# Expert stage of a transformer trunk: two steps of 1792 columns with 7 KB weight units in place of four steps with 8 KB units

## The chip, the core and the metric

One core of a Trainium2 chip runs the whole program. The time is device microseconds of that core from the first to the last work of one execution; lower is better.

## The reference

A small trunk of two layers works on 256 tokens of 1024 numbers, all in float32: a recurrent layer with a dense feed-forward block, then an attention layer with a block of eight experts. Only the expert block is touched by the change:

```python
def moe_swiglu(h, router, w_gate, w_up, w_down):
    logits = (t @ router).astype(jnp.float32)
    top_v, top_i = lax.top_k(logits, TOP_K)                  # TOP_K = 2 of 8
    w = jax.nn.softmax(top_v, axis=-1)
    combine = jnp.sum(jax.nn.one_hot(top_i, N_EXPERTS) * w[..., None], axis=1)
    for e in range(N_EXPERTS):
        out = out + combine[:, e:e + 1] * swiglu(t, w_gate[e], w_up[e], w_down[e])
# swiglu(h, ...) = (silu(h @ w_gate) * (h @ w_up)) @ w_down
# w_gate, w_up: 1024 x 3584 per expert; w_down: 3584 x 1024; 352 MB for all eight
```

## The kernel before

All eight experts' weights are read once, whatever the routing. The experts are sorted by how many tokens chose them and worked on in pairs, one large ("heavy", job 0, up to 128 tokens) beside one small ("light", job 1, up to 64 tokens). There are four such groups here: `OPENING`, `SECOND`, one turn of a loop and `last`. `gather` collects the tokens of a pair by matmuls with one-hot matrices (`xg_hi`, `xg_lo` for the heavy expert, `xl` for the light one), `scatter` adds the weighted results back into `X`.

Weights come in units of 1 MiB (128 partitions x 2048 floats), 42 per expert and 84 per group. SyncE issues the loads (`load`, L461) into a ring of `RING` = 10 slots in an order fixed by `pair_table`; a load waits until TensorE has used up the unit that was in its slot (`used`). A unit of the heavy expert is split: ScalarE copies it rounded into `whi` (`hi_to`, L555, three places), VectorE writes the rest into `lows` (`lo_to`, L1562), and TensorE runs three matmuls per tile, hi x hi, lo x hi and hi x lo (`heavy_unit`, L1380 to L1382). A unit of the light expert is used straight from the ring in full float32; its 64 token columns take half of the array, and the two column halves `g` = 0, 1 alternate (`light_unit`, L1394).

The 3584 hidden columns are done in `PAIRS` = 4 steps of 1024, 1024, 1024 and 512 (`PAIR_W`). Step p computes gate (G) and up (U), multiplies silu(gate) by up (`silu`, `product`), transposes the result on TensorE (`act_transposes` L1356, `light_transposes` L1363, reading every second column through `paired_rows`) and uses it in the down projection (D) of the next step; `act_T_hi` and `act_T_lo` bring the transposes into `aT_hi` and `aT_lo`. Units alternate two light, two heavy (`turns`). In a load of gate or up each partition reads rows of 4 KB (2 KB in the last step), in a load of down 8 KB. The down sums stay in PSUM over the whole group: banks 0 and 1 for the heavy expert, bank 2 for the light one. The heavy gate and up sums use banks 4 and 5, the light ones 6 and 7, the transposes 0, 1, 3, 4 and 5.

At the end of a group `gather` runs for the next one, `light_rows` (L2045) adds the two halves of `xl`, and `y_to_hi` and `y_to_lo` bring the results to SBUF for the scatter.

Of the kernel before, what the change touches and what calls it, by code (L numbers as in the profile page):

```python
# [22 lines left out]
P = 128  # L23
# [31 lines left out]
assert TURNS * RING == PAIR_UNITS + PAIR_UNITS // SKIP and FFN_UNITS % SPLIT == 0  # L55
# [19 lines left out]
PAIRS = 4  # L75
PAIR_W = [2 * CW, 2 * CW, 2 * CW, CW]
PAIR_U = [w // CW * 2 for w in PAIR_W]


def turns(steps, jobs=(1, 0)):  # L80

    for b in range(0, len(steps), RUN):
        for job in jobs:
            for n in steps[b:b + RUN]:
                yield job, n


def pair_table(opening=False):

    units, place = [], {}

    def stage(kind, p, steps, jobs=(1, 0)):
        width = D if kind == "D" else PAIR_W[p]
        tiles = UK * CW // width
        row, col = (p * 2 * UK, 0) if kind == "D" else (0, p * 2 * CW)
        for job, n in turns(steps, jobs):
            place[kind, job, p, n] = len(units)  # L100
            units.append((job, "GUD".index(kind), row + n * tiles, col, width))

    for p in range(PAIRS):
        steps = range(PAIR_U[p])
        if p == 0 and opening:
            for kind, job, few in OPENING_STEPS:
                stage(kind, p, few, (job,))
            continue
        stage("G", p, steps)
        if p:  # L110
            stage("D", p - 1, range(0, 2))
        stage("U", p, steps)
        if p:
            stage("D", p - 1, range(2, PAIR_U[p - 1]))
    stage("D", PAIRS - 1, range(PAIR_U[PAIRS - 1]), (0, 1))
    assert len(units) == PAIR_UNITS == len(place)
    return units, place


OPENING_STEPS = (("G", 0, range(4)), ("G", 1, range(2)), ("U", 0, range(4)), ("G", 1, range(2, 4)),  # L120
                 ("U", 1, range(4)))
# [11 lines left out]
PLACES = (2, 3, 4, 5, 9, 7, 0, 1, 8, 6)  # L133
# [16 lines left out]
class Group:  # L150
# [18 lines left out]
    def unit(self, kind, job, p, n):  # L169
        return self.place[kind, job, p, n % PAIR_U[p]]  # L170
# [5 lines left out]
    def split(self, n):  # L176
        return at(N_MOE + self.ahead * FFN_UNITS + n, FFN_UNITS, self.i)
# [18 lines left out]
HEAVY_DONE = PLACE["D", 0, PAIRS - 1, PAIR_U[PAIRS - 1] - 1] + 1  # L196
# [8 lines left out]
def hybrid_trunk(nc, x, norm_mix, norm_ffn, lru_w_in, lru_conv_w, lru_conv_b, lru_w_a, lru_b_a, lru_w_x, lru_b_x,  # L205
                 lru_log_lambda, lru_w_out, fox_w_in, fox_b_f, fox_q_gain, fox_k_gain, fox_w_out, ffn_w_gate,
                 ffn_w_up, ffn_w_down, moe_router, moe_w_gate, moe_w_up, moe_w_down, out):
    with ExitStack() as ctx:
# [8 lines left out]
        with ExitStack() as w3:  # L217
            ring = sb("ring", [P, RING, UK * CW], where=w3)
        with ExitStack() as w4:
            lows = sb("lows", [P, RING, UK * CW], F32R, where=w4)  # L220
# [6 lines left out]
        with ExitStack() as l3:  # L227
            yl_hi, yl_lo = (sb(s, [P, CW], F32R, where=l3) for s in ("yl_hi", "yl_lo"))
            sb("yl_gap", [P, D], where=l3)
            xl = sb("xl", [P, KT, HD], where=l3)  # L230
        sb("rows3_home", [P, 3 * D])
# [66 lines left out]
        with ExitStack() as a4:  # L298
            with ExitStack() as t4:
                aT_hi = sb("aT_hi", [P, 2, 2 * UK, P], F32R, where=t4)  # L300
                aT_lo = sb("aT_lo", [P, 2, 2 * UK, P], F32R, where=t4)
            sb("aT_home", [P, 4 * D], where=a4)
# [4 lines left out]
            gt = sb("gt", [P, 2 * CW], where=a4)  # L307
            gl = sb("gl", [P, CW], where=a4)
            S = sb("S", [P, TT, 2 * P], F32R, where=a4)
            ST = sb("ST", [P, 2, T], F32R, where=a4)  # L310
            tk = sb("tk", [P, 12, TT, E], where=a4)
            aTl = sb("aTl", [P, 2, 2 * UK, HD], where=a4)
# [16 lines left out]

        def light_T(p):  # L330

            return aTl[:, p % 2, 0:PAIR_W[p] // P].rearrange("p (g a) s -> p a g s", g=2)

        def light_T_bank(p):

            return ps[:, 3, 0:PAIR_W[p] // 2].rearrange("p (a g s) -> p a g s", g=2, s=HD)

# [5 lines left out]

        T_BANK = (0, 4)

# [31 lines left out]
        m_xs, l_silu, l_act, l_T, l_copied = (sem(s) for s in ("m_xs", "l_silu", "l_act", "l_T", "l_copied"))  # L377
# [48 lines left out]
        def _(sp):  # L426
# [28 lines left out]
            def load(group, i, expert):  # L455
                job, matrix, row, col, width = group.table[i]
                tiles = UK * CW // width
                src = expert_w[matrix][expert, row * P:(row + tiles) * P, col:col + width
                                       ].rearrange("o (p k) n -> p (o k) n" if width == D and matrix == 2 else
                                                   "o (k p) n -> p (o k) n", p=P)  # L460
                sp.dma_start(ring[:, slot(i)].rearrange("p (k n) -> p k n", k=tiles), src  # L461
                             ).then_inc(arrived[slot(i)], 16)

            for i in AHEAD:
                n = last_dense(slot(i))
                if slot(i) < RR:
                    sp.wait_ge(lo_done, n)
                else:
                    sp.wait_ge(used, n + 1)
# [66 lines left out]
        def _(act):  # L536
            nxt = [1]

            def hi_to(n, group=None):
# [10 lines left out]
                while nxt[0] < FFN_UNITS and group.heavy[nxt[0]] <= n:  # L550
# [4 lines left out]
                    nc.scalar.activation(whi[:, rounded(q)], ring[:, slot(i)], ACT.Copy).then_inc(hi_done, 1)  # L555
# [239 lines left out]
            def both(bank, n=2 * CW):  # L795
                return ps[:, bank:bank + 2].rearrange("p b n -> p (b n)")[:, 0:n]

# [12 lines left out]
            def y_to_hi(job, done, weighed):  # L810
                act.wait_ge(used, done)
                act.wait_ge(m_ST, weighed)
# [1332 lines left out]
```

## Time and profile before

| | before |
|---|---|
| time, median of 3 (lowest to highest) | 1362.03 us (1360.93 to 1363.13) |
| the profiled execution, its own time | 1364.23 us |
| its span from first to last instruction | 1362.5 us |
| TensorE matmul busy | 97% of the span |
| VectorE, ScalarE busy | 54%, 46% |
| data read from memory | 433 MB |
| granted TensorE clock | 0.998 of full |

The expert stage begins with the first gather at 493 us and ends with the output at 1362 us. Matmuls are pipelined, so one of 390 ns can start every 227 ns; a distance between starts is read from the first column of the timeline, a busy time includes the overlap only once.

### The profile page before, as it was taken

Reading aid. Unit: us, or ns where it says so; the run is one execution under the profiler, and the core shown is the slowest. Engines: PE = TensorE matmul, PEld = TensorE weight load, DVE = VectorE, ACT = ScalarE, POOL = GpSimd, SP = SyncE. Lnnn points to the kernel's source line nnn. Section 1 sums busy time; section 2 is a strip of 40 time slices with the busy share of each in tenths; the row PEclk is TensorE's granted clock in tenths of the full one; section 3 lists DMA queues with packets and bytes.
Section 4 is the critical chain, followed back from the end, with each engine's and each line's share of the span. In section 5 each row is a group of like instructions: output and inputs, shape, how many; then the busy total and the mean of one; then the engine's idle time right before and its main releaser. Section 6 shows DMA issues by size and latency. Waiting matters only on the chain.

```text
span 1362.5 us, 16077 instructions
## 1 busy us (share of the span) xinstructions
PE 1324.5 (97%) x6430; PEld 935.8 (69%) x6430; DVE 736.3 (54%) x632; ACT 629.7 (46%) x573; POOL 29.0 (2%) x34
## 2 busy tenths in 40 slices
PE   9999999999999999999999999999999999999998
PEld 8978888888888875565666556575556656665665
DVE  6975444445654574554555554555545555455455
ACT  5855334444456463434444444444444444453443
POOL 2000000000310000000000000000000000000000
PEclk9999999999999999999999999999999999999999
DMA  9556555654543449999999999999999999999995
GB/s 333 170 181 218 192 192 189 193 189 126 184 144 124 164 173 366 414 415 410 403 413 409 393 413 413 405 412 409 403 409 412 407 411 409 411 400 414 411 401 230
DMA packets 127881, 434.79 MB, mean 319 GB/s; under 512 B 6960, under 2 KB 9120, under 8 KB 113472
## 3 DMA queue, kind: packets, MB, share of 16 engines
q1 hardware_dynamic: 127344, 433.11, 82.9%
q8 instruction: 51, 0.84, 0.3%
q0 software_dynamic: 368, 0.63, 0.2%
q14 instruction: 22, 0.18, 0.0%
q10 hardware_dynamic: 96, 0.03, 0.0%
HBM read 432.69 MB, written 1.05 MB: 318 GB/s over the span
## 4 chain that ended last, share of the span: by engine, by line
PE 73%; DMA 15%; DVE 5%; ACT 4%; issue 1%; SPq 1%; DVEq 0%; POOL 0%; ACTq 0%
PE ps L1394 15%; DMA ring<-in_moe_w_gate_dram 9%; PE ps L918 9%; PE ps L920 9%; PE ps L919 9%; PE ps L1380 9%; PE ps L1381 8%; PE ps L1382 8%; DMA ring<-in_moe_w_up_dram 4%; DVE lows L1562 2%; DMA ring<-in_moe_w_down_dram 2%; ACT whi L555 2%; PE ps L1325 1%; DVE wlo L1555 1%; SPq L461 1%
## 5 line engine op out<-in xcount | busy, mean ns | idle before, releaser
L1562 DVE TENSOR_TENSOR lows<-ring,whi 128x2048 fp32r<-128x2048 f32 x168 | 383.1, 2290 | 256.9 <-ACT whi L555 256.8
L555 ACT ACTIVATE whi<-ring 128x2048 fp32r<-128x2048 f32 x168 | 320.3, 1912 | 324.5 <-DMA ring<-in_moe_w_up_dram 120.7
L1394 PE MATMUL ps<-ring,xl 128*64 128x512 f32 (+1 forms) x1024 | 204.1, 544 | 5.0 <-DVE xl L2045 3.4
L1555 DVE TENSOR_TENSOR wlo<-raw,whi 128x2048 fp32r<-128x2048 f32 x73 | 166.5, 2288 | 73.9 <-PE ps L920 71.8
L1380 PE MATMUL ps<-whi,hT_hi 128*128 128x512 f32 x444 | 179.3, 404 | 13.5 <-DVE lows L1562 13.0
L547 ACT ACTIVATE whi<-raw 128x2048 fp32r<-128x2048 f32 x73 | 139.4, 1917 | 85.9 <-PE ps L920 82.9
L1381 PE MATMUL ps<-lows,hT_hi 128*128 128x512 f32 x444 | 173.3, 390 | 0.0
L1382 PE MATMUL ps<-whi,hT_lo 128*128 128x512 f32 x444 | 173.0, 390 | 0.0
L918 PE MATMUL ps<-whi,hT_hi 128*128 128x512 f32 x384 | 152.9, 398 | 3.2 <-DVE wlo L1555 1.4
L920 PE MATMUL ps<-whi,hT_lo 128*128 128x512 f32 x384 | 149.7, 390 | 0.0
L919 PE MATMUL ps<-wlo,hT_hi 128*128 128x512 f32 x384 | 149.5, 389 | 0.0
L1394 PEld LDWEIGHTS ps<-ring,xl 128*64 128x64 f32 x1024 | 69.1, 136 | 116.0 <-issue 107.9
L1380 PEld LDWEIGHTS ps<-whi,hT_hi 128*128 128x128 f32 x444 | 83.3, 188 | 67.4 <-issue 26.4
L1394 PE MATMUL ps<-ring,aTl 128*64 128x512 f32 x448 | 102.3, 598 | 0.0
L1380 PE MATMUL ps<-whi,aT_hi 128*128 128x512 f32 x224 | 91.2, 407 | 5.7 <-DVE lows L1562 5.7
L1382 PEld LDWEIGHTS ps<-whi,hT_lo 128*128 128x128 f32 x444 | 83.3, 188 | 18.0
L1381 PEld LDWEIGHTS ps<-lows,hT_hi 128*128 128x128 f32 x444 | 83.5, 188 | 15.2
L1382 PE MATMUL ps<-whi,aT_lo 128*128 128x512 f32 x224 | 87.6, 391 | 0.0
L1381 PE MATMUL ps<-lows,aT_hi 128*128 128x512 f32 x224 | 87.4, 390 | 0.0
L918 PEld LDWEIGHTS ps<-whi,hT_hi 128*128 128x128 f32 x384 | 72.2, 188 | 19.0 <-issue 3.1
L920 PEld LDWEIGHTS ps<-whi,hT_lo 128*128 128x128 f32 x384 | 72.1, 188 | 15.3
L919 PEld LDWEIGHTS ps<-wlo,hT_hi 128*128 128x128 f32 x384 | 72.2, 188 | 13.8
(318 smaller groups left out, 1318.7 us busy)
## 6 DMA issues: line engine op xcount, KB each, us to landing
ring<-in_moe_w_gate_dram SPq DMA_DIRECT2D x112, 1024.0 KB, 11.9
ring<-in_moe_w_up_dram SPq DMA_DIRECT2D x112, 1024.0 KB, 13.4
ring<-in_moe_w_down_dram SPq DMA_DIRECT2D x112, 1024.0 KB, 13.9
raw<-in_fox_w_in_dram SPq DMA_DIRECT2D x16, 1024.0 KB, 5.2
raw<-in_ffn_w_gate_dram SPq DMA_DIRECT2D x14, 1024.0 KB, 5.2
raw<-in_ffn_w_up_dram SPq DMA_DIRECT2D x14, 1024.0 KB, 5.1
raw<-in_ffn_w_down_dram SPq DMA_DIRECT2D x14, 1024.0 KB, 5.1
raw<-in_lru_w_in_dram SPq DMA_DIRECT2D x8, 1024.0 KB, 10.2
```

The lines of the kernel that those rows point to most:

```text
L461: sp.dma_start(ring[:, slot(i)].rearrange("p (k n) -> p k n", k=tiles), src).then_inc(arrived[slot(i)], 16)
L547: nc.scalar.activation(whi[:, m % HR], raw[:, m % RR], ACT.Copy).then_inc(hi_done, 1)
L555: nc.scalar.activation(whi[:, rounded(q)], ring[:, slot(i)], ACT.Copy).then_inc(hi_done, 1)
L918: mm(dst(t), hi, whi[:, m % HR, k * CW:(k + 1) * CW], start=first and k == 0, stop=False)
L919: mm(dst(t), hi, wlo[:, m % LR, k * CW:(k + 1) * CW], start=False, stop=False)
L920: ins = mm(dst(t), lo, whi[:, m % HR, k * CW:(k + 1) * CW], start=False, stop=last and k == UK - 1)
L1380: mm(ps[:, bank + h], hi, w_hi[:, cols], start=first and k == 0, stop=False)
L1381: mm(ps[:, bank + h], hi, w_lo[:, cols], start=False, stop=False)
L1382: ins = mm(ps[:, bank + h], lo, w_hi[:, cols], start=False, stop=last and k == tiles - 1)
L1394: ins = mm(ps[g * HD:(g + 1) * HD, bank, 0:half], src(k), ring[:, slot(i), cols], start=first and k == 0, stop=last and k == tiles - 1, sk ...
L1555: nc.vector.tensor_tensor(wlo[:, m % LR], raw[:, m % RR], whi[:, m % HR].bitcast(F32), ALU.subtract).then_inc(lo_done, 1)
L1562: nc.vector.tensor_tensor(lows[:, slot(i)], ring[:, slot(i)], whi[:, rounded(q)].bitcast(F32), ALU.subtract).then_inc(lo_done, 1)
```

## The change

The hidden columns are done in `PAIRS` = 2 steps of `WIDE` = 1792. Every unit has 7 KB per partition (`ring` is 11 slots x 1792 floats): 48 units per expert, 96 per group. A gate or up unit is one tile of 128 rows x 1792 columns, so each partition reads one run of 7 KB. For down, a partition takes seven neighbouring rows of 896 (28 KB in one piece), and a unit is a quarter of it; the activations are therefore transposed at every seventh column (`every_seventh`) in place of every second.

Gate and up of the heavy expert fill four banks with 448 columns each (4 to 7), the light expert uses 2 and 3. Down matmuls are cut at bank and unit edges (`down_pieces`): three of 512 columns and one of 256 per unit. Since the light banks are shared, the light down sums are brought to SBUF three times in a group and added up in `yl` by VectorE (`light_sum`). The order of units, of the waits and of VectorE's and ScalarE's operations around them is written anew. `light_rows` moves into the last down step. `ST`, `gl`, `aT_hi` and `aT_lo` get new places in SBUF.

```diff
-PAIR_UNITS = 2 * FFN_UNITS
-RING, SPLIT, RUN = 10, 3, 2
-SKIP = 14
+PAIRS = 2
+NU = 8
+WIDE = F // PAIRS
+HALF = WIDE // 2
+BW = WIDE // 4
+RW = HALF // P
+EXPERT_UNITS = PAIRS * 3 * NU
+PAIR_UNITS = 2 * EXPERT_UNITS
+RING, SPLIT, RUN = 11, 3, 2
+SKIP = 32
...
+def down_pieces(u):
+    cuts = [u * WIDE, (u + 1) * WIDE] + [c for c in range(0, RW * D, CW) if u * WIDE < c < (u + 1) * WIDE]
+    edges = sorted(set(cuts))
+    return [(c // D, c % D, e - c, c - u * WIDE) for c, e in zip(edges, edges[1:])]
...
+        stage("G", 0, range(NU), HEAVY_FIRST)
+        stage("U", 0, range(NU), HEAVY_FIRST)
+    stage("G", 1, range(NU), LIGHT_FIRST)
+    stage("D", 0, DOWN_A, LIGHT_FIRST)
+    stage("U", 1, range(NU), HEAVY_FIRST)
+    stage("D", 0, DOWN_B, HEAVY_FIRST)
+    stage("D", 1, range(NU), HEAVY_FIRST)
...
             def load(group, i, expert):
+                if kind == "D":
+                    rows = p * WIDE + n // 4 * HALF
+                    src = w[expert, rows:rows + HALF, :].rearrange("o (q r) n -> q (o r n)", r=RW)
+                    src = src[:, n % 4 * WIDE:(n % 4 + 1) * WIDE]
+                else:
+                    src = w[expert, n * P:(n + 1) * P, p * WIDE:(p + 1) * WIDE].rearrange("o p n -> p (o n)")
...
-            def paired_rows(src, a):
-                return src[:, a // 2 * 2 * P:(a // 2 + 1) * 2 * P].rearrange("p (q two) -> p two q", two=2)[:, a % 2]
+            def every_seventh(src, b, a):
+                return src[:, b * HALF:(b + 1) * HALF].rearrange("p (q r) -> p r q", r=RW)[:, a]
...
+                for h in range(4):
+                    cols = slice(h * BW, (h + 1) * BW)
+                    dst = ps[:, 4 + h, 0:BW]
+                    mm(dst, xg_hi[:, n], w_hi[:, cols], start=n == 0, stop=False)
+                    mm(dst, xg_hi[:, n], w_lo[:, cols], start=False, stop=False)
+                    ins = mm(dst, xg_lo[:, n], w_hi[:, cols], start=False, stop=n == NU - 1)
...
+            def light_down(group, p, n):
+                for a, c, width, at_col in down_pieces(n % 4):
+                    g = c // CW
+                    ins = mm(ps[g * HD:(g + 1) * HD, 2 + p, c % CW:c % CW + width], aTl[:, in_half(p, b), a],
+                             ring[:, slot(i), at_col:at_col + width], start=a == 0 and (p == 0 or b == 0),
+                             stop=a == RW - 1 and (p == 0 or b == 1), skip_group_check=True)
...
+            def light_sum(group, part):
+                p, n = ((0, DOWN_A[-1]), (0, DOWN_B[-1]), (1, NU - 1))[part]
+                dve.wait_ge(used, group.units(group.unit("D", 1, p, n) + 1))
+                if part == 0:
+                    nc.vector.tensor_copy(yl[:], ps[:, 2]).then_inc(l_sum, 1)
+                else:
+                    dve.wait_ge(l_sum, group.nth(part, 3))
+                    nc.vector.tensor_tensor(yl[:], ps[:, 2 + p], yl[:], ALU.add).then_inc(l_sum, 1)
...
+                lo_to(unit("G", 0, 1, 0), group)
+                act_T_lo(group, 0)
+                if group is not OPENING:
+                    accumulate(1, group)
+                    lo_to(unit("G", 0, 1, 5), group)
+                    if following is not None:
+                        one_hot(group)
+                lo_to(unit("D", 0, 0, 2), group)
+                light_sum(group, 0)
+                lo_to(unit("D", 0, 0, 4), group)
+                product(group, 1)
+                light_product(group, 1)
+                lo_to(unit("D", 0, 0, 6), group)
+                act_T_lo(group, 1)
+                lo_to(unit("D", 0, 1, 1), group)
+                light_sum(group, 1)
+                if following is not None:
+                    lo_to(unit("D", 0, 1, 4), group)
+                    light_rows(following)
```

## Rows read from the trace of the kernel before

**Rows 1.** The page: busy times of the engines and the 40 slices.
```profile
PE 1324.5 (97%) x6430; PEld 935.8 (69%) x6430; DVE 736.3 (54%) x632; ACT 629.7 (46%) x573; POOL 29.0 (2%) x34
DMA  9556555654543449999999999999999999999995
```
**Rows 2.** Four stretches between gathers: from:to, length, PE busy (instructions), clock, DMA share, GB/s.
```profile
493.29:697.00 203.71, 196.50 (x922) 1.00 1.00 394
697.00:912.42 215.42, 209.66 (x972) 1.00 1.02 408
912.42:1128.60 216.18, 210.42 (x975) 1.00 1.02 408
1128.60:1357.00 228.40, 222.62 (x1032) 1.00 0.97 386
```
**Rows 3.** Waits of PE from 540 us on, and of ACT from 759 to 975.
```profile
PE ps L1380 <- DVE lows L1562: 18.7, 23, 1.4
PE ps L1394 <- DVE xl L2045: 3.4, 2, 1.7
...
ACT whi L555 <- DMA ring<-in_moe_w_up_dram: 30.2, 10, 6.2
ACT whi L555 <- DMA ring<-in_moe_w_down_dram: 25.6, 10, 5.5
ACT whi L555 <- DMA ring<-in_moe_w_gate_dram: 22.6, 8, 6.0
```
**Rows 4.** Stretches by packet size (2, 2, 8, 8, 4 KB): busy times, clock, share, GB/s.
```profile
861.00:869.00 8.00, 8.00 (x42) 4.96 (x39) 5.68 (x3) 4.03 (x4) 0.00 (x0) 1.00 1.05 387
884.00:892.00 8.00, 7.14 (x36) 4.97 (x34) 3.77 (x2) 1.80 (x2) 0.00 (x0) 1.00 1.06 389
872.00:880.00 8.00, 7.71 (x50) 5.66 (x47) 4.59 (x2) 3.19 (x3) 0.00 (x0) 1.00 1.02 420
897.00:913.00 16.00, 15.74 (x73) 10.80 (x73) 9.89 (x7) 8.42 (x6) 0.00 (x0) 1.00 1.01 418
936.00:964.00 28.00, 28.00 (x127) 16.39 (x126) 14.71 (x13) 10.95 (x8) 0.00 (x0) 1.00 1.03 409
```
**Rows 5.** Timeline of PE: start us, length us, instruction; dense 512, light 512/256, gather.
```profile
724.08 0.50 PE L1380 MATMUL ps<-whi,hT_hi 128*128 128x512 f32 x1
724.42 0.40 PE L1381 MATMUL ps<-lows,hT_hi 128*128 128x512 f32 x1
...
860.76 3.65 PE L1394 MATMUL ps<-ring,aTl 128*64 128x512 f32 x16
...
871.51 3.67 PE L1394 MATMUL ps<-ring,xl 128*64 128x256 f32 x32
...
878.07 0.39 PE L1382 MATMUL ps<-whi,hT_lo 128*128 128x512 f32 x1
...
880.79 0.39 PE L1382 MATMUL ps<-whi,hT_lo 128*128 128x512 f32 x1
...
912.42 2.08 PE L1316 MATMUL ps<-S,hn_hi 128*128 128x256 f32 x16
914.34 0.40 PE L1380 MATMUL ps<-whi,aT_hi 128*128 128x512 f32 x1
```
**Rows 6.** Transposes, step 1 (L960) and 2 (L1356): loads min/median/max ns; then starts.
```profile
L960 PEld LDWEIGHTS ps<-ident,X x48: 138/141/148, 87.8 to 482.4; 128*128 128x128 f32 x48
L1356 PEld LDWEIGHTS ps<-ident,gt x112: 195/209/219, 539.1 to 1342.0; 128*128 128x128 f32 x112
...
481.90 0.49 PE L960 MATMUL ps<-ident,X 128*128 128x128 f32 x3
482.01 0.49 PE L960 MATMUL ps<-ident,X 128*128 128x128 f32 x3
...
867.82 0.52 PE L1356 MATMUL ps<-ident,gt 128*128 128x128 f32 x3
867.94 0.52 PE L1356 MATMUL ps<-ident,gt 128*128 128x128 f32 x3
```
**Rows 7.** Groups by shape (busy us, mean ns), 759 to 975; then one wait of PE.
```profile
L1562 DVE TENSOR_TENSOR lows<-ring,whi 128x2048 fp32r<-128x2048 f32 x42 | 95.7, 2290 | 64.4 <-ACT whi L555 64.4
L2026 DVE TENSOR_TENSOR gt<-gt,ps 128x1024 f32<-128x1024 f32 x3 | 3.7, 1222 | 12.8 <-PE ps L1382 12.8
L2039 DVE TENSOR_TENSOR gl<-gl,ps 128x512 f32<-128x512 f32 x3 | 2.1, 685 | 2.3 <-PE ps L1394 2.3
L2045 DVE TENSOR_TENSOR xl<-ps,xl 128x512 f32<-128x512 f32 x1 | 0.7, 683 | 0.0
...
979.69 0.50 PE L1380 MATMUL ps<-whi,hT_hi 128*128 128x512 f32 x1 [1.33 <-DVE lows L1562]
```

More of the change, by code:

```diff
@@ L549, in hi_to @@
                     return
-                while nxt[0] < FFN_UNITS and group.heavy[nxt[0]] <= n:
+                while nxt[0] < EXPERT_UNITS and group.heavy[nxt[0]] <= n:
                     q, i = nxt[0], group.heavy[nxt[0]]
@@ new lines, in heavy_down @@
+            def heavy_down(group, p, n):
+                i = group.unit("D", 0, p, n)
+                b = n // 4
+                w_hi, w_lo = heavy_halves(group, i)
+                pe.wait_ge(lo_done, group.split(group.heavy.index(i)))
+                for a, c, width, at_col in down_pieces(n % 4):
+                    hi, lo = aT_hi[:, in_half(p, b), a], aT_lo[:, in_half(p, b), a]
+                    cols = slice(at_col, at_col + width)
+                    dst = ps[:, c // CW, c % CW:c % CW + width]
+                    mm(dst, hi, w_hi[:, cols], start=p == b == a == 0, stop=False, skip_group_check=True)
+                    mm(dst, hi, w_lo[:, cols], start=False, stop=False, skip_group_check=True)
+                    ins = mm(dst, lo, w_hi[:, cols], start=False, stop=p == b == 1 and a == RW - 1,
+                             skip_group_check=True)
+                ins.then_inc(used, 1)
@@ L1496, in pair @@
-                pe.wait_ge(l_copied, group.nth(PAIRS, PAIRS))
-                pe.wait_ge(m_tlo, group.nth(PAIRS, PAIRS))
-                if following is not None:
-                    gather(following, 0)
-                for job, n in turns(range(2), (0, 1)):
-                    down_unit(group, job, PAIRS - 1, n)
-                    if following is not None and job == 0 and n == 0:
+                    first_step(group)
+                act_transposes(group, 0)
+                light_transposes(group, 0)
@@ new lines, in pair @@
+                if group is not OPENING:
+                    pe.wait_ge(m_acc, group.twice(1))
+                    scatter(1)
+                for job, n in turns(range(NU), LIGHT_FIRST):
+                    if n == 0:
+                        pe.wait_ge((m_tlo, l_copied)[job], group.nth(1, PAIRS))
+                    half_unit(group, "G", job, 1, n)
+                    if group is not OPENING and job == 1 and n == 5:
+                        pe.wait_ge(m_acc, group.twice(2))
+                        selection_transposes(group)
@@ new lines, in pair @@
+                for job, n in turns(DOWN_B, HEAVY_FIRST):
+                    if job == 1 and n == DOWN_B[0]:
+                        pe.wait_ge(l_copied, group.nth(2, PAIRS))
+                    down_unit(group, job, 0, n)
+                    if (job, n) == (0, DOWN_B[0]):
+                        light_transposes(group, 1)
+                    if (job, n) == (0, DOWN_B[1]):
+                        act_transposes(group, 1)
+                pe.wait_ge(m_tlo, group.nth(2, PAIRS))
+                for job, n in turns(range(NU), HEAVY_FIRST):
+                    down_unit(group, job, 1, n)
+                    if following is not None and (job, n) == (0, 1):
+                        gather(following, 0)
+                    if following is not None and (job, n) == (0, 3):
@@ L1558, in lo_to @@
                     return
-                while nxt[0] < FFN_UNITS and group.heavy[nxt[0]] <= n:
+                while nxt[0] < EXPERT_UNITS and group.heavy[nxt[0]] <= n:
                     q, i = nxt[0], group.heavy[nxt[0]]
@@ L2104, in _ @@
-            pair(SECOND, Group(0, 2))
+            pair(OPENING, None, SECOND)
+            pair(SECOND, OPENING, Group(0, 2))
             dve.wait_ge(counted, 1)
@@ L2107, in _ @@
             with dve.Fori(0, loops) as n:
-                pair(Group(n, 2), Group(n, 3))
+                pair(Group(n, 2), Group(n, 1), Group(n, 3))
             last = Group(loops, 2)
-            pair(last, None)
-            for job in range(2):
-                y_to_lo(job, last.twice(1 + job))
+            pair(last, Group(loops, 1), None)
+            y_to_lo(0, last.twice(1))
+            light_sum(last, 2)
+            y_to_lo(1, last.twice(2))
             for j in range(2):
```

462 lines of the change are left out of this document (199 added, 263 removed).

## The prediction

> **What bounds the kernel now.** I read the page first. TensorE is busy 97% of the span, and from about 530 us the DMA slices stand at 9 to the end [rows 1]. The reader should see two resources near their limit in the same stretch, the expert stage. So I split the stage at the four places where TensorE begins to gather for a pair of experts, and ask for busy time, DMA share and GB/s [rows 2]. The middle stretches take 215.4 and 216.2 us; TensorE works 209.7 and 210.4 of them and the DMA engines all of it, at 408 GB/s. The idle time of TensorE in the four stretches is 7.2 + 5.8 + 5.8 + 5.8 = 24.6 us. The waits name what ends it: 18.7 us of the whole span for `lows`, 3.4 us for `xl` [rows 3]. ScalarE's waits say who was behind most of the `lows`: in one period it waits 78 us for weights to land [rows 3]. So the stage runs at the DMA's pace, but a DMA that costs nothing could give back 24.6 us and no more: behind it stands TensorE with 210 us of work in 216.
>
> **The DMA side.** A unit is 1 MiB now, in packets of 4 KB per partition for gate and up, 2 KB in step 3, 8 KB for down. The rate goes with the packet [rows 4]: 387 to 389 GB/s where 2 KB packets land, 409 for 4 KB, 418 to 420 for 8 KB. One engine moves 64 KB of a unit: 2.70 us at 388 GB/s, 2.565 at 409. The 16 packets more cost 0.14 to 0.16 us, near 9.5 ns each, over a floor of 2.41 us; 8 packets would then take 2.49 us, 421 GB/s, as the rows show. A group has 48 gate/up units at 2.565, 8 at 2.71 and 28 down at 2.49: 214.5 us, near the measured 216. After the change there are 96 units of 7/8 the size, 8 packets each: 2.41 x 7/8 + 0.076 = 2.185 us, so 209.8 us a group. The weights come 4.7 us sooner, and the DMA falls just below TensorE's present work.
> The Trainium skill ("DMA: Bandwidth & Descriptors", Why small descriptors are slow) gives about 3 cycles of fixed overhead per packet. At its 850 MHz, 480 packets fewer per engine and group would save an estimated 1.7 us, not 4.7. The rows show nearly three times that overhead, and the sum goes by the rows.
>
> **What TensorE gains as work.**
> (a) Heavy units. The same columns go through, but gate and up in 448-column matmuls, and down in 512s with a 256 at a unit's edge. Dense 512-column matmuls start 2.72 us / 12 = 226.7 ns apart, 256-column ones (the gather) 1.92 / 16 = 120 ns [rows 5]. That is 0.417 ns a column plus 13.3 ns each. Matmuls of the heavy expert go from 504 to 576 a group, 288 more in all: 288 x 13.3 ns = +3.8 us.
> (b) Switches between the two experts. The first matmul after a switch costs 0.1 us extra (724.08 to 724.42 against 0.23; [rows 5]). 40 switches become 45 per group: 20 x 0.1 = +2.0 us.
> (c) Light units. 16 instructions of 512 columns and 32 of 256 take the same 3.6 us [rows 5], so a narrower piece is free as long as the two column halves alternate. In down, eight cuts a group put two 256-column pieces on the same half one after the other. The trace has no such pair. If nothing overlaps there, one piece of 256 costs 0.21 us more, 8 x 4 x 0.21 = 6.8 us; the other end is 0. I take the middle, +3.4 us, having nothing nearer.
> (d) Transposes. There are 42 per group before and after, 168 in all. The operand that is loaded is read at every second column now, at every seventh afterwards. Rows exist for a step of 1 and of 2 [rows 6]: the load takes 141 and 209 ns, and starts of transposes lie 0.11 and 0.12 us apart, since the load hides behind its neighbour. A step of 7 is in no row. Below: 0 (a step of 2 already reads one number at a time; nothing suggests a gain). Above: the load grew by 67 ns on the doubling from 1 to 2; if the next doubling costs 134 and then no more, the load takes 343 ns and is what paces: +134 ns x 168 = 22.5 us. I take 20 ns each, +3.4 us, near the lower end, because the starts moved by only 10 ns when the load grew by 67.
> (e) Tail. The small expert's last sum now passes VectorE before ScalarE reads it (`light_sum`, 512 columns): +0.7 us by the 512-column `xl` addition [rows 7], with nothing beside it at the end.
> What stays: the gathers, the scatters, the number of transposes, the front up to 493 us. The waits for `xl` go (3.4 us of the 24.6): `light_rows` moves from the end of the group to the middle of the last down step, some 10 us before TensorE needs it.
>
> **What stays as waiting.** VectorE's operations get longer. By its 1024- and 512-column rows (1222 and 685 ns, [rows 7]) one of 1792 columns takes 2.03 us, and a `lows` unit shrinks from 2.29 to 2.02. I laid out its queue at the three seams. After step 0 the product (2.03), the light product (1.09), one `lows` and `act_T_lo` fit under the two light units (3.1), the transposes (2.4) and the scatter (2.4): slack of a microsecond, where it costs 1.33 us now (the wait at 979.69, [rows 7]). In the first down half `light_sum` (0.7) stands ahead of a `lows` (2.02) that is due in 2.4 us: 0.3 late. In the second half the same chain is even with its due time, and `act_T_lo` makes the last `lows` 0.4 late. That is about 1 us a group, 4 in all. The DMA, 3.2 us a group below TensorE's new work, adds perhaps 0.5 in three groups and 1 in the opening, where the landed units are used up first: 6.5 us remain of the 24.6.
>
> **The sum.** -24.6 + 6.5 + 3.8 + 2.0 + 3.4 + 3.4 + 0.7 = -4.8 us. The profiled execution took 1364.2 us (span 1362.5), 2.2 above the median. 1364.2 - 4.8 = 1359.4; against the median of 1362.0, 1357.2 us. A middle group should take 209.9 + (3.8 + 2.0 + 3.4 + 3.4)/4 + 1.5 = 214.5 us.
>
> **Rivals.**
> B, the slower side: the step of 7 sets the pace of the transposes. Place: `act_transposes` and `light_transposes`, all on TensorE, which nothing covers. It decides against the change from about 50 ns per transpose. At 134 ns: 1357.2 + 22.5 - 3.4, less 2.5 of waits that the slower TensorE no longer meets: 1373.8 us, and 1377 with (c) in full. For it: the load already rose by 67 ns at a step of 2, to well above the 120 ns between starts. Against it: that rise hardly moved the starts.
> The Trainium skill ("SBUF — State Buffer", Specifications, the row on cachelines) says that at least two hits per 16-byte line are needed for full bandwidth. A step of 2 floats still has two hits, a step of 7 (28 bytes) one. By that rule B holds; the trace doesn't settle it, as its load rows slow down already where the rule says full bandwidth.
> C: VectorE or ScalarE becomes late at the seams, since long operations stand ahead of `lows` with slack near zero. 2.5 us more a group: 1367. Against it: both engines are only half busy [rows 1].
> D: (c) and (d) cost nothing and 3 us less waiting stays: 1357.2 - 6.8 - 3 = 1347.4.
> E, the change doesn't do what it says: 7 KB packets move no faster than the mix now (a 28 KB pitch between partitions, in no row). The period stays 216 with TensorE's additions inside it: 1363. Against it: the steady order 388, 409, 419 by packet size.
>
> **How the numbers follow.** Chances: A (the forecast) 0.42, B 0.30, C 0.08, D 0.10, E 0.10. Range: D's 1347.4 to B with (c) in full, 1377, a microsecond more for an error of the sum: 1347 to 1378, which leaves out the ends of B and D and unforeseen waits. A measurement of this kernel can tell about 0.2%, 2.7 us, from no change. A spreads from 1352 to 1363: 0.32 faster, 0.09 same, 0.01 slower. D is faster (0.10); E is same (0.09) or slower (0.01); C and B are slower (0.37), 0.01 of B same. Together: faster 0.42, same 0.19, slower 0.39. Both signs hold much; A's own range is 1352 to 1363.
>
> **What would show it.** DMA side right: packets of 7 KB alone, 418 to 421 GB/s wherever the queues are full, and a DMA share under 1.00 in the middle stretches. (a): heavy starts 200 ns apart. (c): 16 light instructions in 3.14 us, a down pair up to 0.2 us longer at each cut. (d): the load of `gt` near 209 to 230 ns and starts near 0.12 to 0.14 us, or for B above 300 ns and 0.25 us. Waits of TensorE: no `xl`, `lows` under 2 us a group. The forecast is wrong if TensorE's work in a middle stretch leaves 212 to 215 us, or if the share of the DMA stays at 1.02 over 216 us.

## The result and the profile after

| | before | after |
|---|---|---|
| median (lowest to highest), 20 runs each | 1362.55 us (1360.88 to 1366.74) | 1364.89 us (1364.55 to 1366.27) |
| after / before, with its 95% interval | | 1.0018 [1.0011, 1.0025] |
| span of the profiled execution | 1362.5 us | 1363.1 us |

The kernel after is 0.18% slower. Its interval lies above 1, so the direction is clear of noise, but it is too little to matter: the prediction took 0.2% as what can be told from no change. The forecast was 1357.2 us, 0.35% faster. Behind the small number two large ones cancel. The page of the kernel after shows it first (busy times; the chain that ended last; the landing of the weight loads in us); [rows 1] has before:

```profile
PE 1346.0 (99%) x6782; PEld 986.7 (72%) x6782; DVE 744.3 (55%) x644; ACT 630.1 (46%) x565; POOL 28.9 (2%) x34
...
PE 92%; DVE 4%; ACT 2%; DMA 1%; issue 1%; SPq 0%; DVEq 0%; ACTq 0%
...
ring<-in_moe_w_gate_dram SPq DMA_DIRECT2D x128, 896.0 KB, 8.4
ring<-in_moe_w_up_dram SPq DMA_DIRECT2D x128, 896.0 KB, 8.9
ring<-in_moe_w_down_dram SPq DMA_DIRECT2D x128, 896.0 KB, 10.1
```

TensorE works 1346.0 us where it worked 1324.5: 21.5 us more, in a span that hardly moved. The stretches between gathers say where. They answer [rows 2]; the boundary is the first matmul of the gather, and the first and last stretch have other ends than before, since the gather now stands in another place among the down units. Columns: from:to, length, TensorE busy (instructions), granted clock, DMA share, GB/s.

```profile
492.44:675.93 183.49, 181.32 (x912) 1.00 0.99 401
675.93:892.35 216.42, 216.32 (x1065) 1.00 1.01 411
892.35:1108.79 216.44, 216.34 (x1065) 1.00 1.00 408
1108.79:1357.80 249.01, 248.53 (x1213) 1.00 0.93 378
```

The four lengths sum to 865.4 us, against 863.7 before. The idle time of TensorE in them is 2.2 + 0.1 + 0.1 + 0.5 = 2.9 us, against 24.6: 21.7 us of waiting went. Its work is 862.5 us, against 839.2: 23.3 us of work came. A middle group has 216.3 us of work where it had 209.7 and 210.4, and idles for 0.1 us. Its length, 216.4 us, is within 1 us of what it was (215.4 and 216.2). The waits of TensorE from 540 us on, which answer [rows 3], are down to two; `lows` and `xl` are gone:

```profile
PE ps L1434 <- ACT aTl L879: 1.7, 1, 1.7
PE ps L1369 <- DVE yl_lo L2068: 0.4, 1, 0.4
```

The DMA did what was forecast. Two stretches in which its queues were full (all five engines' busy times, clock, share, GB/s), beside [rows 4]:

```profile
604.00:612.00 8.00, 8.00 (x40) 5.27 (x40) 3.96 (x2) 5.04 (x4) 0.00 (x0) 1.00 1.02 422
618.00:640.00 22.00, 22.00 (x108) 15.68 (x108) 12.54 (x7) 10.21 (x6) 0.00 (x0) 1.00 1.02 419
```

7 KB packets move at 419 to 422 GB/s, where 418 to 421 was forecast. Over a whole group it is 408 to 411. That is TensorE's pace: a group's 88.1 MB in its 216.4 us are 407 GB/s, and a load waits until TensorE has freed its slot.

So the question is why TensorE has 5.9 to 6.7 us more work in a middle group, where the forecast had 3.15. The timeline has the answer in two places. Gate and up, then down; each time 16 instructions of the light expert (two units) and the first matmul of the heavy one behind them. A matmul of the light expert leaves two records in the trace, so x16 are eight matmuls:

```profile
631.40 3.23 PE L1434 MATMUL ps<-ring,xl 128*64 128x448 f32 x16
634.56 0.47 PE L1422 MATMUL ps<-whi,hT_hi 128*128 128x448 f32 x1
...
639.62 3.23 PE L1434 MATMUL ps<-ring,xl 128*64 128x448 f32 x16
...
688.33 3.65 PE L1464 MATMUL ps<-ring,aTl 128*64 128x512 f32 x16
691.91 0.50 PE L1451 MATMUL ps<-whi,aT_hi 128*128 128x512 f32 x1
...
696.98 3.65 PE L1464 MATMUL ps<-ring,aTl 128*64 128x512 f32 x16
```

Two light units of gate or up take 634.56 - 631.40 = 3.16 us. Two light units of down take 691.91 - 688.33 = 3.58 us, for the same 7 KB each. It is what two units of 8 KB took before, x16 and 3.65 us long in [rows 5] too. A whole turn (two light, two heavy) is 639.62 - 631.40 = 8.22 us for gate and up and 696.98 - 688.33 = 8.65 us for down. The turn before was 9.25 us (light blocks at 785.28 and 794.53 in its timeline), and 7/8 of that is 8.09.

### The profile page after: what moved, and what is told of

Read it like the earlier page. It is cut to its first block, busy times and chain, and to the rows that moved or that the text cites. A ratio compares the mean times of both kernels' runs of the same rounds, so it can differ in the third digit from the quotient of the medians.

```text
span 1363.1 us, 16877 instructions
## 1 busy us (share of the span) xinstructions
PE 1346.0 (99%) x6782; PEld 986.7 (72%) x6782; DVE 744.3 (55%) x644; ACT 630.1 (46%) x565; POOL 28.9 (2%) x34
## 4 chain that ended last, share of the span: by engine, by line
PE 92%; DVE 4%; ACT 2%; DMA 1%; issue 1%; SPq 0%; DVEq 0%; ACTq 0%
PE ps L1434 15%; PE ps L962 9%; PE ps L964 8%; PE ps L963 8%; PE ps L1464 8%; PE ps L1422 8%; PE ps L1424 8%; PE ps L1423 8%; PE ps L1451 4%; PE ps L1452 4%; PE ps L1453 4%; PE ps L1369 1%; PE ps L1399 1%; DMA raw<-in_lru_w_in_dram 1%; DVE wlo L1613 1%; PE ps L1360 1%
## 5 line engine op out<-in xcount | busy, mean ns | idle before, releaser
L1620 DVE TENSOR_TENSOR lows<-ring,whi 128x1792 fp32r<-128x1792 f32 x192 | 386.2, 2023 | 270.6 <-ACT whi L603 270.4
L603 ACT ACTIVATE whi<-ring 128x1792 fp32r<-128x1792 f32 x192 | 324.4, 1698 | 296.0 <-PE ps L1424 130.8
L1434 PE MATMUL ps<-ring,xl 128*64 128x448 f32 x1024 | 205.9, 545 | 1.7 <-ACT aTl L879 1.7
L1422 PE MATMUL ps<-whi,hT_hi 128*128 128x448 f32 x508 | 191.7, 377 | 0.0
L1424 PE MATMUL ps<-whi,hT_lo 128*128 128x448 f32 x508 | 185.6, 365 | 0.0
L1423 PE MATMUL ps<-lows,hT_hi 128*128 128x448 f32 x508 | 185.5, 365 | 0.0
L962 PE MATMUL ps<-whi,hT_hi 128*128 128x512 f32 x384 | 152.9, 398 | 3.2 <-DVE wlo L1613 1.4
L964 PE MATMUL ps<-whi,hT_lo 128*128 128x512 f32 x384 | 149.7, 390 | 0.0
L1464 PE MATMUL ps<-ring,aTl 128*64 128x512 f32 (+1 forms) x512 | 116.7, 545 | 0.0
L1451 PE MATMUL ps<-whi,aT_hi 128*128 128x512 f32 (+1 forms) x256 | 97.6, 381 | 0.4
```

What stands on the lines that cost most here:

```text
L603: nc.scalar.activation(whi[:, rounded(q), 0:WIDE], ring[:, slot(i)], ACT.Copy).then_inc(hi_done, 1)
L962: mm(dst(t), hi, whi[:, m % HR, k * CW:(k + 1) * CW], start=first and k == 0, stop=False)
L964: ins = mm(dst(t), lo, whi[:, m % HR, k * CW:(k + 1) * CW], start=False, stop=last and k == UK - 1)
L1422: mm(dst, xg_hi[:, n], w_hi[:, cols], start=n == 0, stop=False)
L1423: mm(dst, xg_hi[:, n], w_lo[:, cols], start=False, stop=False)
L1424: ins = mm(dst, xg_lo[:, n], w_hi[:, cols], start=False, stop=n == NU - 1)
```

## The experiments

Every kernel was timed beside the kernel before on the same chip; ratios are to those runs. "The changed kernel" is the one under test, 1.0018. The edits are shown in part; "..." marks what is left out.

**Theory 1: narrow beside wide.** The prediction's step (c) spoke of 256-column pieces on the same half of the array one behind the other. The first theory was that a lone piece, which has no neighbour of its own length, costs the 0.44 us. `alt_halves` orders the light pieces so that the halves alternate all through, by a table `light_pieces` that cuts one 512 more in each pair of units in two:

```diff
-                for a, c, width, at_col in down_pieces(n % 4):
+                for a, c, width, at_col in light_pieces(n % 4):
...
```

> The changed kernel with only the order and cutting of the light expert's down matmuls altered: beside each 256-column piece its partner on the other column half is cut to 256 too, so that halves of equal width alternate; columns, sums and loads are the same. Theory 1 (a 256-column piece beside a 512-column one on the other half costs as much as a 512-column one, 0.44 us per cut, 32 cuts): a light down pair falls from 3.58 to 3.14 us, a middle group from 216.4 to about 213, the whole by 13 to 14 us, to a ratio near 0.992 against the kernel before. If the DMA (209.8 us a group) takes over part, 0.994. Rival (the extra TensorE work lies in the 448-column matmuls and the switches, the cut is nearly free): the pair stays above 3.5 us and the ratio at 1.001 to 1.002.

Measured: 1365.95 us, ratio 1.0014 [1.0005, 1.0023]. The pair (now nine matmuls, x18) takes 605.40 - 601.82 = 3.58 us as before the edit:

```profile
601.82 3.65 PE L1473 MATMUL ps<-ring,aTl 128*64 128x512 f32 x18
605.40 0.50 PE L1460 MATMUL ps<-whi,aT_hi 128*128 128x512 f32 x1
```

Theory 1 fell: this order of the pieces, in which the halves alternate, changes nothing. What is left is how many columns each half gets. A partition's quarter of 28 KB is 1792 floats, 1.75 rows of 1024, and two units are 3.5 rows. Columns 0 to 511 of a row go to half 0, columns 512 to 1023 to half 1. So one half gets four pieces of 512 in a pair of units and the other three, and in the next pair it is the other way round. **Theory 2:** a block of light matmuls lasts as long as the half with more columns. Then 4 x 512 columns in one half cost what the pairs of 2048-column units cost before (4 x 512 in both halves), 3.58 us; balanced, it would be 7/8 of that, 3.13. That is 0.44 us x 8 pairs x 4 groups = 14 us.

**Turns of four.** Over four light down units both halves get seven pieces of 512, so theory 2 says 6.3 us in place of 7.16. `alt_run4` makes all turns four units long, gate and up too, on top of the edit of `alt_halves`:

```diff
-RING, SPLIT, RUN = 11, 3, 2
+RING, SPLIT, RUN = 11, 3, 4
```

> The same as alt_halves, and units of one expert follow each other in runs of four in place of two (the one constant RUN). Theory 1 with switches at 0.1 us each: about 22 switches fewer per group, 88 in all, 9 us below alt_halves if the units land in time; the DMA's 209.8 us a group is then the next limit, so a middle group of 210 to 211 us and a ratio near 0.987. Rival: four heavy units in a row outrun ScalarE and VectorE (1.70 and 2.02 us a unit against 2.43) or the DMA, waits for the lower halves return, and it is no faster than alt_halves or slower.

Measured: 1390.4 us, ratio 1.0199 [1.0184, 1.0213]. The block behaves as theory 2 says (`828.95 6.24`, 36 instructions), but TensorE now waits for VectorE and ScalarE, whose operations were laid out for turns of two, and behind the longest waits the granted clock falls as well (0.66 from 790 to 800 us; 0.984 over the whole run).

```profile
PE ps L1460 <- DVE lows L1629: 20.7, 11, 2.8
PE ps L1443 <- ACT aTl L888: 14.8, 4, 4.1
...
828.95 6.24 PE L1473 MATMUL ps<-ring,aTl 128*64 128x512 f32 x36
```

`down_quads` takes turns of four light units in down only:

```diff
-def turns(steps, jobs):
+def turns(steps, jobs, run=RUN):
...
+def downs(steps, jobs):
+    if len(steps) == 4:
+        return list(turns(steps, jobs, 4)) if jobs == LIGHT_FIRST else [(0, 4), (0, 5), (1, 4), (1, 5), (1, 6), (1, 7),
+                                                                        (0, 6), (0, 7)]
+    return [(0, 0), (0, 1), (1, 0), (1, 1), (1, 2), (1, 3), (0, 2), (0, 3), (0, 4), (0, 5), (1, 4), (1, 5), (1, 6),
+            (1, 7), (0, 6), (0, 7)]
...
```

> The changed kernel, with the light expert's down units taken four in a row (a whole half of a step) in place of two; the loads follow the same new order, gate and up keep their pairs. Two down units are 3.5 rows of 1024 columns, so one column half of the array gets four 512-column matmuls and the other three, in the next pair the other way round; four units give seven to each. Theory 2 (the extra TensorE work in down is this imbalance, paid in full since the longer half sets the pace): light down takes 6.2 us for four units in place of 2 x 3.58, 1.0 us less four times a group, with the fewer switches 4 us a group; the whole 10 to 16 us faster than the change, ratio 0.990 to 0.994 against the kernel before, if no new wait comes. Theory 1 (narrow pieces) has already fallen. Rival: waits for the heavy lower halves or for landed units return with four in a row, and the ratio stays above 0.998.

Measured: 1369.51 us, ratio 1.0057 [1.0043, 1.0071], the wrong way. TensorE's work fell (1337.6 us against 1346.0), but in three of the groups it waits twice for a `lows`, 14.4 us in all, and behind five of these six waits the clock falls. Waits of TensorE, three windows of 10 us (clock last but two), and its timeline:

```profile
PE ps L1431 <- DVE lows L1629: 7.4, 3, 2.5
PE ps L1460 <- DVE lows L1629: 7.0, 3, 2.3
...
680.00:690.00 10.00, 10.00 (x57) 7.81 (x55) 3.09 (x2) 1.52 (x2) 0.00 (x0) 1.00 1.02 419
690.00:700.00 10.00, 7.65 (x33) 4.91 (x33) 7.14 (x5) 6.76 (x5) 0.00 (x0) 0.83 0.98 381
1130.00:1140.00 10.00, 7.65 (x40) 4.55 (x40) 8.47 (x5) 6.40 (x4) 0.00 (x0) 1.00 0.79 286
...
693.89 0.39 PE L1460 MATMUL ps<-whi,aT_hi 128*128 128x256 f32 x1 [2.35 <-DVE lows L1629]
...
695.28 0.63 PE L1461 MATMUL ps<-lows,aT_hi 128*128 128x512 f32 x1
695.71 0.63 PE L1462 MATMUL ps<-whi,aT_lo 128*128 128x512 f32 x1
...
696.56 0.63 PE L1461 MATMUL ps<-lows,aT_hi 128*128 128x512 f32 x1
696.99 0.63 PE L1462 MATMUL ps<-whi,aT_lo 128*128 128x512 f32 x1
```

From 695.28, 1.4 us after the wait, a matmul of 512 columns starts every 0.43 us in place of 0.23: the lower of the two clock levels. The granted clock of the window is 0.83. The third of the waits of 2.35 us, which ends at 1133.64, had no such fall: 1.00 from 1130 to 1140.

`quads_reordered` mends the place of the waits. In the last down step all heavy units but two stand before the last four light ones, and the next group's tokens come in one heavy unit later:

```diff
-    return [... (0, 4), (0, 5), (1, 4), (1, 5), (1, 6), (1, 7), (0, 6), (0, 7)]
+    return [... (0, 4), (0, 5), (0, 6), (0, 7), (1, 4), (1, 5), (1, 6), (1, 7)]
...
-                    hi_to(unit("D", 0, 1, 4), group)
+                    hi_to(unit("D", 0, 1, 5), group)
...
-                    lo_to(unit("D", 0, 1, 4), group)
+                    lo_to(unit("D", 0, 1, 5), group)
```

> down_quads with its seams mended: the last down step takes its heavy units as 2, then 6 in a row, and ends with four light ones again, and ScalarE and VectorE bring in the next pair's tokens after one heavy unit more, so that no heavy half waits behind them. Theory 2 (imbalance of the column halves, 1.0 us per four light down units): a middle group of 212 to 213 us in place of 216.4, no idle stretch above 1 us and so no fall of the granted clock; the whole 12 to 16 us below the change, ratio 0.990 to 0.993. Rival: six heavy units in a row meet late lower halves or late landings, and the ratio is 0.996 or more.

Measured: 1345.09 us, ratio 0.9875 [0.986, 0.989]. It beats both kernels. No wait for `lows` is left, and four light units take 680.67 - 674.46 = 6.21 us where two pairs took 7.16:

```profile
674.46 6.28 PE L1473 MATMUL ps<-ring,aTl 128*64 128x512 f32 x32
680.67 0.50 PE L1460 MATMUL ps<-whi,aT_hi 128*128 128x512 f32 x1
...
672.46:884.04 211.58, 211.58 (x1063) 1.00 1.01 419
```

A middle group is 211.6 us, 4.85 less than 216.4. Theory 2 explains 4 x 0.95 = 3.8 of it, and four blocks of the light expert in place of eight save eight switches between the experts, at 0.1 us 0.8. Since this kernel also changes the order of units, two more runs separate the causes.

**Balance alone.** `balanced_halves` leaves order, loads and turns, and deals the light columns to the halves in chunks of 256 by turns, so that a pair gives seven chunks to each (its columns come out in another order, another sum):

```diff
-                for a, c, width, at_col in down_pieces(n % 4):
-                    g = c // CW
-                    ins = mm(ps[g * HD:(g + 1) * HD, 2 + p, c % CW:c % CW + width], aTl[:, in_half(p, b), a],
-                             ring[:, slot(i), at_col:at_col + width], start=a == 0 and (p == 0 or b == 0),
+                for k in range(RW):
+                    a, c = divmod(n % 4 * RW + k, 4)
+                    g, half = c % 2, c // 2
+                    ins = mm(ps[g * HD:(g + 1) * HD, 2 + p, half * 2 * P:(half + 1) * 2 * P], aTl[:, in_half(p, b), a],
+                             ring[:, slot(i), k * 2 * P:(k + 1) * 2 * P],
+                             start=a == 0 and half == 0 and (p == 0 or b == 0),
```

> The changed kernel with one edit: the light down units are cut into seven pieces of 256 columns each, and the pieces go to the two column halves by turns (piece k of a quarter to half k mod 2), so that two units of a pair give 7 pieces to either half. Loads, order of units, waits and all heavy work stay. The light down results stand in another order of columns, so the output is another sum. Theory 2 (the longer half sets the pace: now 4 x 512 columns against 3 x 512 in each pair): the light down pair falls from 3.58 to 3.14 us, 8 pairs x 4 groups x 0.44 = 14 us less, ratio 0.991 to 0.992, middle group 212.9 us, and it takes half of what was gained by taking the down units in fours out of the comparison: the rest there is order and switches. Rival (a light unit of 7 KB costs this much however its columns stand, for instance by the ring read or by the switch of weights): pair stays at 3.58 and the ratio at 1.001 to 1.002.

Measured: 1352.64 us, ratio 0.9921 [0.9908, 0.9935]: the median is 12.3 us below that of the changed kernel, against 14 expected (12.0 below `seam_move`, timed beside it, which is as slow as the changed kernel). The pair falls to 690.45 - 687.27 = 3.18 us:

```profile
687.27 3.24 PE L1465 MATMUL ps<-ring,aTl 128*64 128x256 f32 x28
690.45 0.50 PE L1451 MATMUL ps<-whi,aT_hi 128*128 128x512 f32 x1
...
675.14:888.47 213.33, 213.24 (x1160) 1.00 1.01 417
```

A middle group falls by 3.1 us, to 213.3. 8 x (3.58 - 3.18) = 3.2. Theory 2 holds; the rival, that a 7 KB unit costs this much however its columns stand, fell. The narrower pieces are not what gives it: in gate and up 32 records of 256 columns and 16 of 512 take the same [rows 5], and the turns of four have pieces of 512.

**Seam alone.** `seam_move` makes only the second and third edit of `quads_reordered`.

> The changed kernel with one edit: at the last down stage ScalarE and VectorE bring in the next group's tokens one heavy unit later (after heavy unit 5 in place of 4), as in the kernel with down units in fours and their order mended. Order of units, matmuls and loads stay. The changed kernel waits only 2.9 us in the expert stage, none of it for these operations, so theory 2 expects no change: ratio 1.001 to 1.002 and a middle group of 216.4 us. Rival (the order of these operations is what gave the gain of the mended fours over the plain ones by itself): a gain of 1 us or more per group, ratio 0.999 or below.

Measured: 1364.68 us, ratio 1.0014 [1.0005, 1.0023]. The seam edit gives nothing by itself (a middle group is 216.4 us still), so the gain of `quads_reordered` over the changed kernel is in the order and length of the blocks.

**What the DMA costs.** Two kernels load only half of the columns of the small expert's units and multiply that half twice, so their results are another sum; the work of the engines stays. `before_thin` does it to the kernel before, `after_thin` to the changed one.

```diff
+                dst = ring[:, slot(i)]
+                if job == 1:
+                    dst, src = dst[:, 0:HALF], src[:, 0:HALF]
+                sp.dma_start(dst, src).then_inc(arrived[slot(i)], 16)
```

> The kernel before, with every load of the light expert carrying half its bytes (its matmuls read the loaded half twice, so part of the weights is left out); matmuls, waits and operations are the same in number and size. The DMA's work falls by a quarter, so what is left is TensorE with the waits that the DMA does not cause. Theory 1 (24.6 us of idle TensorE, of which all but the 1.3 us at each seam of ScalarE and VectorE come from landing): 1342 to 1346 us, ratio 0.985 to 0.988. Rival (the waits are made by the order on ScalarE and VectorE): above 1355 us.

> The changed kernel, with every load of the light expert carrying half its bytes (its matmuls read the loaded half twice, so part of the weights is left out). The same was measured on the kernel before: 22.5 us less. Theory (TensorE alone sets the pace of the change, 2.9 us of it idle in the expert stage): 0 to 3 us less than the change, so a ratio of 1.000 to 1.002, and about 22 us slower than the kernel before with the same thinning. Rival (the DMA still shares the pace): 6 us or more less than the change, below 0.998.

Measured: `before_thin` 1341.14 us, ratio 0.9835 [0.982, 0.985]; `after_thin` 1365.48 us, ratio 1.0023 [1.0013, 1.0034]. The DMA cost the kernel before 22.5 us (1363.61 beside it), and costs the changed one nothing that can be measured. The same stretches of `before_thin` (columns as in the result) show where they were:

```profile
492.61:689.60 196.99, 195.29 (x918) 1.00 0.85 304
689.60:900.42 210.82, 209.40 (x975) 1.00 0.87 315
900.42:1111.13 210.71, 209.38 (x976) 1.00 0.87 313
1111.13:1334.03 222.90, 221.58 (x1031) 1.00 0.79 288
```

The four are 841.4 us long, 22.3 less. Idle time went from 24.6 to 5.8 us (5.3 of it waits for `lows`, one of 1.3 in each group), so 18.7 of the 24.6 were the DMA's. The other 3.6 us went from TensorE's busy time, 839.2 to 835.6, though the matmuls are the same (in `after_thin` the same edit left it at 863 us): in the kernel before, the DMA also stretched what counts as work.

**Transposes.** `unit_step` reads neighbouring columns in place of every seventh, so the down projection gets the activations in another order (another sum).

```diff
-                return src[:, b * HALF:(b + 1) * HALF].rearrange("p (q r) -> p r q", r=RW)[:, a]
+                return src[:, b * HALF:(b + 1) * HALF].rearrange("p (r q) -> p r q", r=RW)[:, a]
```

> The changed kernel, with the transposes reading neighbouring columns in place of every seventh. This orders the activations otherwise than the down rows, so it is a timing experiment that computes another sum. Theory 1 (the step does not pace the transposes; loads took 216 ns against 209 at a step of 2): the load falls to 140 ns, the starts from about 0.12 to 0.11 us, the whole by at most 168 x 0.015 = 2.5 us. Rival B of the prediction in its full size would give back 20 us.

Measured: 1363.77 us, ratio 1.0001 [0.9992, 1.001], 1.1 us below the changed kernel's median, 2.3 by the ratios. The loads of `gt` (min/median/max ns) and a block of 14 transposes, the changed kernel first, then `unit_step` with a middle group:

```profile
L1399 PEld LDWEIGHTS ps<-ident,gt x112: 197/216/221, 563.2 to 1307.6; 128*128 128x128 f32 x112
...
873.24 1.87 PE L1399 MATMUL ps<-ident,gt 128*128 128x128 f32 x14
```

```profile
L1399 PEld LDWEIGHTS ps<-ident,gt x112: 138/140/143, 564.2 to 1306.1; 128*128 128x128 f32 x112
...
873.21 1.69 PE L1399 MATMUL ps<-ident,gt 128*128 128x128 f32 x14
...
676.18:891.98 215.80, 215.70 (x1063) 1.00 1.01 412
```

In the kernel before, at a step of 2:

```profile
867.71 1.11 PE L1356 MATMUL ps<-ident,gt 128*128 128x128 f32 x8
```

Against a step of 1, a step of 7 costs 76 ns a load, of which little reaches the end: a middle group is 0.6 us shorter in `unit_step`, 2.5 us over four groups, 15 ns a transpose. But the change went from a step of 2, not of 1, to 7. With the last transpose 0.28 us long, starts lie (1.11 - 0.28) / 7 = 119 ns apart at a step of 2 and (1.87 - 0.29) / 13 = 122 at 7, 0.5 us over 168 transposes. A load takes 209 ns at a step of 2 [rows 6] and 216 at 7. The Trainium skill ("SBUF — State Buffer", Specifications) asks for two hits per 16-byte line for full bandwidth, which a step of 2 floats still has and a step of 7 hasn't. The rows don't agree: 141, 209 and 216 ns for steps of 1, 2 and 7, so 68 of the 75 ns are lost between 1 and 2.

**The width of 448.** Dense matmuls of 448 columns start 202.6 ns apart (618.23 to 622.89, 23 intervals), 2.6 ns more than the line through 256 and 512. `banks_512` cuts the heavy gate and up columns into three 512s and one 256:

```diff
-                    cols = slice(h * BW, (h + 1) * BW)
-                    dst = ps[:, 4 + h, 0:BW]
+                    cols = slice(h * CW, min((h + 1) * CW, WIDE))
+                    dst = ps[:, 4 + h, 0:cols.stop - cols.start]
```

> The changed kernel with the heavy gate and up sums filling four banks as 512, 512, 512 and 256 columns in place of four times 448; the number of matmuls, the columns and all loads are the same. In the change, 448-column matmuls start 202.6 ns apart, where the line through 256 and 512 columns gives 200. Theory 3 (a matmul of 448 carries 2.6 ns more than that line): 1536 such matmuls, 4 us less, ratio 0.997 to 0.999. Rival (only the number of matmuls counts): no change, 1.001 to 1.002.

Measured: 1363.72 us, ratio 1.0011 [1.0002, 1.0021]. The interval overlaps that of the changed kernel, so it is undecided whether anything is gained. By the trace a middle group goes from 216.4 to 216.2 us and a turn from 8.22 to 8.21 us, where the 2.6 ns would have been worth 1.0 us a group. The width of 448 isn't a cause worth naming; where the 2.6 ns come from is open.

**Both together.** `quads_and_512` is `quads_reordered` with `banks_512`; `quads_thin` is the same with half of the small expert's bytes.

> quads_reordered and banks_512 together. If both theories hold and the DMA's 209.8 us a group does not bind: a middle group of 211 to 212 us, ratio 0.987 to 0.991, faster than both kernels. If the DMA binds from 212 us on, no better than quads_reordered.

> The kernel of quads_and_512 (down units of the small expert in fours, heavy gate and up columns in 512s), with one edit: the loads of the small expert bring only half of the columns, and its matmuls read that half again; its results are another sum. It asks what bounds that version, where TensorE works all of a middle group (211.3 us) and the DMA engines move 419 GB/s in all of it. If TensorE alone sets the pace: ratio 0.986 to 0.988, middle group 211.3 us, as with full loads. If the DMA already holds it back in part (a unit is awaited without a visible wait of TensorE, or the opening group starts late): the time falls below that, ratio 0.985 or less.

Measured: `quads_and_512` 1343.8 us, ratio 0.9868 [0.9853, 0.9883], the fastest, though not separable from `quads_reordered`. `quads_thin` 1344.25 us, ratio 0.9863 [0.9845, 0.988]. A middle group of `quads_and_512` is 211.3 us with TensorE busy in all of it, while the DMA moves 419 GB/s. With half of the small expert's bytes, the time is the same. TensorE alone sets the pace even there. The margin of the DMA is thin, though, by an estimate: a group's 88.1 MB at 419 GB/s take 210.2 us.

## Why the prediction was wrong

**What bounds the kernel before: right in size, in part by luck.** The DMA held TensorE, and `before_thin` gains 22.5 us, under the 24.6 that the prediction gave as the most. But 5.8 us of the idle time were not the DMA's, and 3.6 us of its cost stood in TensorE's busy time, which the prediction took as work that stays. The changed kernel lost 21.7 us of idle time.

**The DMA side: right.** 419 to 422 GB/s where 418 to 421 was forecast. The sign named with it, a DMA share under 1.00 in the middle stretches, told nothing: the share stood at 1.00 and 1.01 although the GB/s fell to 408 and 411. The GB/s are the column to read.

**(a) and (b), cutting and switches: right in kind, about half of the size.** 5.8 us were forecast for both. The turn for gate and up is 8.22 us against 8.09 for 7/8 of the old one, 0.12 to 0.13 us too much; 24 turns a group make 3.0 us, 12 us over four groups. Per turn, three more matmuls at 13.3 ns give 0.04, the eighth of two switches that isn't saved 0.025, the light pair 0.03 (3.16 against 3.13). What makes up the rest is open; `banks_512` shows that it isn't the width.

**(c), light cuts: the step that failed.** The sum took 3.4 us, with 6.8 as its upper end; measured is 12.3 us (`balanced_halves`), 14.3 by the timeline (32 pairs at 3.58 us in place of 7/8 of 3.58). The step priced a 256-column piece whose neighbour stands on the same half, and it took for granted that the halves stay balanced. It looked at the order of pieces inside a unit and never added up the columns that each half gets in a block. The diff gave the numbers (512 + 512 + 512 + 256 in one unit, with bank edges at every 512), and [rows 5] gave the price of 4 x 512 a half: 3.6 us. The upper bound was therefore no bound.

**(d), transposes: small, as forecast.** 3.4 us forecast, about 0.5 from a step of 2 to one of 7 by the starts; the whole step from 1 to 7 is 2.5. Rival B, 22.5 us, fell. Starts lie 0.12 us apart, as named beforehand.

**(e), tail: half hidden.** 0.7 us were forecast, with nothing beside it. The last sum does take 0.69 us on VectorE, but TensorE's last scatters of the heavy expert run beside it; TensorE then waits 0.4 us for `yl_lo`.

**What stays as waiting: too dark.** 6.5 us were forecast, 2.9 stayed, and no wait for `lows` at the seams. Rival C fell. That changed with the experiments: `down_quads` and `alt_run4` moved blocks and met just these waits.

**Rivals D and E.** D fell with (c). E gave 1363 us, the nearest of all to 1364.9, but for a reason that is not so: it let the DMA stay slow.

**The sum again.** With measured terms for the stage: -21.7 (idle time; what was left of (e) is in it) - 3.6 (busy time that went with the DMA's hold) + 12 (a, b) + 14.3 (c) + 0.5 (d) = +1.5 us. The stage measured +1.7 and the medians +2.3. Term (c) decided the sign: with the forecast's 3.4 in its place this sum is -9.4, and `balanced_halves`, which differs from the changed kernel only in this, is faster than the kernel before. The term for (a) and (b) was 6 us too small as well, but three others made up for it with 11 us on the other side: the waits that stayed, with (e) among them (4.3), (d) (2.9), and the 3.6 us of busy time that no term had. A forecast of 1366.1, which 12.3 for (c) alone would have given, would have been near by that luck. The sign of failure that the prediction named for TensorE's work, a middle stretch outside 212 to 215 us, came: 216.3.

## What to carry to other kernels

Where small matmuls share the array in column halves, add up the columns of each half from switch to switch: the block lasts as long as the fuller half. Here a pair of units that isn't a whole number of rows unbalanced it, and another order of the pieces in the pair didn't help. When a change moves a bound from the DMA to TensorE, every term of TensorE's work, free until then or not, counts in full; price the new layout block by block with the timeline's own blocks. A stall may cost more than its length: behind five of six waits of 2.35 to 2.5 us in `down_quads` the clock fell. So regroup units and move the waits of their helpers together.

## What the runs showed of the hardware

- Light matmuls (64 token columns, one half of the array): 4 x 512 columns in one half and 3 x 512 in the other take 3.58 us, as long as 4 x 512 in both; 7 x 256 in each take 3.18 us. Seven and seven pieces of 512 take 6.21 us.
- Loading a stationary operand of float32 at a step of 1, 2 and 7 columns takes 140, 209 and 216 ns. The transposes that use it start 109, 119 and 122 ns apart.
- Full rate with 7 KB packets at a pitch of 28 KB between partitions: 419 to 422 GB/s.
- In `down_quads` the clock was at full speed until TensorE waited 2.35 us, and at half from 1.4 us after it; 0.83 was granted in that window. Behind one other wait of 2.35 us it stayed at 1.00. In the kernel before, waits of 1.3 us went with a granted clock of 1.00.
- The DMA's hold on TensorE shows in its busy time too: the same matmuls took 839.2 us of busy time in the kernel before and 835.6 in `before_thin`.
